# Delta rule with the keys convolved first, corner products and 32x32 transposes in its triangular inverse, and weight quarters set between the levels

## What is computed

```
proj = rms_norm(x) @ w_in                      # q, k, v, z, gates a and b, attention, index heads
qkv = silu(causal_short_conv(g_qkv, conv_w))   # 3072 channels, 4 taps
gq = l2_normalize(gq) * 128 ** -0.5 ; gk = l2_normalize(gk)
a_mat = where(strict, (k * beta) @ k.T * decay, 0)
sol = triangular_solve(a_mat + I, [v * beta, k * beta * exp(g_cum)])
qk = where(incl, q @ k.T * decay, 0)
v_new = u - w @ state ; o = q_dec @ state + qk @ v_new
state = state * exp(g_last) + k_dec.T @ v_new  # from chunk to chunk
o_gdn = rms_norm(o) * silu(z) ; merged = sigmoid(gate_a) * o_gdn + sigmoid(gate_b) * o_att
x = x + merged @ w_out
```

## Time and profile before

| | us |
|---|---|
| median of 3 runs (lowest to highest) | 950.84 (950.75 to 953.18) |
| the profiled execution | 952.35 |
| its span, first to last instruction | 950.5 |
| PE busy in it | 921.4 |
| DVE, ACT, POOL busy | 591.9, 451.3, 124.7 |

### The profile page before, as it was taken

The page is one execution under the profiler, slowest core; times in us unless marked ns, Lnnn a source line. Parts: engine busy times, 40 slices in busy tenths (PEclk is TensorE's granted clock), DMA queues, the critical chain, the costliest instruction groups (busy, mean ns, idle before and its releaser), DMA issues.

```text
span 950.5 us, 11857 instructions
## 1 busy us (share of the span) xinstructions
PE 921.4 (97%) x4691; PEld 771.8 (81%) x4691; DVE 591.9 (62%) x816; ACT 451.3 (47%) x654; POOL 124.7 (13%) x82
## 2 busy tenths in 40 slices
PE   8999999998998999999999999999998999999998
PEld 5887788876996888888887889888887888888886
DVE  4469978979456656654445745877774655555542
ACT  5265355963344544453335434753553455454531
POOL 0322112676601000000000002100000000000100
PEclk9999999999998999999999999999999999999999
DMA  7774542432312555555567645343541556554561
GB/s 268 191 247 137 177 133 89 143 124 70 95 45 85 164 193 178 177 177 177 179 192 276 208 143 174 138 133 120 181 144 44 165 164 196 183 177 133 200 221 67
DMA packets 83138, 149.87 MB, mean 158 GB/s; under 512 B 8320, under 2 KB 16048, under 8 KB 82960
## 3 DMA queue, kind: packets, MB, share of 16 engines
q1 hardware_dynamic: 79424, 144.52, 46.9%
q10 hardware_dynamic: 3040, 3.79, 1.1%
q0 software_dynamic: 624, 0.87, 0.8%
HBM read 147.72 MB, written 1.44 MB: 157 GB/s over the span
## 4 chain that ended last, share of the span: by engine, by line
PE 84%; DVE 7%; ACT 4%; DMA 3%; issue 1%; POOL 0%; SPq 0%; DVEq 0%; ACTq 0%
PE gemm L477 23%; PE gemm L479 23%; PE gemm L478 23%; PE mixbank L720 2%; DMA raw<-in_w_in_dram 2%; PE mixbank L612 2%; PE mixbank L587 2%; DVE w_lo L1482 1%; PE mixbank L493 1%; ACT w_hi L1019 1%; ACT junk L1175 1%; PE mixbank L825 1%; PE mixbank L598 1%; DVE mix L1599 1%; ACT mix L1187 1%
## 5 line engine op out<-in xcount | busy, mean ns | idle before, releaser
L1482 DVE TENSOR_TENSOR w_lo<-raw,w_hi 128x2048 fp32r<-128x2048 f32 (+3 forms) x131 | 287.6, 2209 | 177.5 <-ACT w_hi L1019 177.4
L477 PE MATMUL gemm<-w_hi,s_hi 128*128 128x512 f32 (+3 forms) x912 | 354.6, 389 | 11.8 <-DVE w_lo L1482 7.6
L479 PE MATMUL gemm<-w_hi,s_lo 128*128 128x512 f32 (+3 forms) x912 | 347.3, 381 | 0.0
L478 PE MATMUL gemm<-w_lo,s_hi 128*128 128x512 f32 (+3 forms) x912 | 347.1, 381 | 0.0
L1019 ACT ACTIVATE w_hi<-raw 128x2048 fp32r<-128x2048 f32 (+3 forms) x140 | 255.4, 1836 | 167.7 <-DMA raw<-in_w_in_dram 47.6
L477 PEld LDWEIGHTS gemm<-w_hi,s_hi 128*128 128x128 f32 x912 | 172.4, 189 | 46.5 <-issue 10.6
L479 PEld LDWEIGHTS gemm<-w_hi,s_lo 128*128 128x128 f32 x912 | 172.3, 189 | 32.9
L478 PEld LDWEIGHTS gemm<-w_lo,s_hi 128*128 128x128 f32 x912 | 172.6, 189 | 31.0 <-issue 0.5
L2165 POOL TENSOR_TENSOR sm<-sm 128x2 f32<-128x2 f32 (+4 forms) x14 | 29.1, 2077 | 514.4 <-DVE sm L1526 318.8
L2159 POOL TENSOR_TENSOR w_lo<-raw,w_hi 128x2048 fp32r<-128x2048 f32 x9 | 41.4, 4616 | 202.4 <-ACT w_hi L1019 202.4
L477 PE MATMUL gemm<-w_hi,hT_hi 128*128 128x512 f32 x128 | 50.6, 396 | 0.0
(11 more groups left out here) (300 smaller groups left out, 950.8 us busy)
## 6 DMA issues: line engine op xcount, KB each, us to landing
raw<-in_w_in_dram SPq DMA_DIRECT2D x40, 1024.0 KB, 5.1
raw<-in_w_mlp_up_dram SPq DMA_DIRECT2D x16, 1024.0 KB, 5.6
raw<-in_w_mlp_down_dram SPq DMA_DIRECT2D x16, 1024.0 KB, 5.1
raw<-in_w_gate_dram SPq DMA_DIRECT2D x10, 1024.0 KB, 5.1
raw<-in_w_up_dram SPq DMA_DIRECT2D x10, 1024.0 KB, 5.2
raw<-in_w_down_dram SPq DMA_DIRECT2D x10, 1024.0 KB, 5.2
raw<-in_w_out_dram SPq DMA_DIRECT2D x8, 1024.0 KB, 5.1
raw<-in_w_xkv_dram SPq DMA_DIRECT2D x8, 1024.0 KB, 5.2
```

The costliest lines, as they stand in the source:

```text
L477: nc.tensor.matmul(o, hi, wh, start=kt == 0, stop=False)
L478: nc.tensor.matmul(o, hi, wl, start=False, stop=False)
L479: last = nc.tensor.matmul(o, lo, wh, start=False, stop=kt == blk["kt"] - 1)
L1482: V.tensor_tensor(w_lo[:, s, 0:kn, 0:width], raw[:, s, 0:kn, 0:width], w_hi[:, s, 0:kn, 0:width].bitcast(F32), ALU.subtract)\
```

## The change

**Convolution.** `CONV_ORDER` puts the keys first, with a table of banks. The loop is written out. Decay rows are made early by PE (with a constant that gives the differences at once), the exponential is taken by ACT from PSUM, and POOL applies the mask. The turned keys are copied by DVE (`keys`), and ACT squares the copies. Queries aren't turned back: ACT squares them as they are, and 16 products with one column each sum them (`query_sums`). DVE makes `AT` (`inverse_rows`) amid the taps of v. The norm factors of the queries are a power of their own (`gdnq`).

```
+        CONV_ORDER = (4, 5, 6, 7, 0, 1, 2, 3, 8, 9, 10, 11)
+        CONV_BANK, DEC_BANK = (0, 1, 2, 0, 2, 1, 0, 2, 0, 2, 1, 2), (1, 0, 2, 1)
+        KK_BANK, KQ_BANK = (1, 3, 0, 3), (0, 1, 2, 0)
+        BACK_ORDER = (0, 1, 2, 3, 8, 9, 10, 11)
...
+            def turned_back(i):
+
+                s = BACK_ORDER[i]
+                e = CONV_ORDER[s]
+                pe.wait_ge(sem("gdn_y"), s + 1)
...
+            def query_sums():
+
+                pe.wait_ge(sem("gdn_q2"), 4)
+                pe.wait_ge(sem("gdn_at"), 4)
+                for p in range(4):
+                    for j in range(2):
+                        for t in range(NT):
+                            c = 8 * t + 2 * p + j
+                            last = nc.tensor.matmul(M[3][:, c:c + 1], Y2[:, p, j, P * t:P * t + P], cst[:, C_ONES:C_ONES + 1], start=True, stop=True)
+                last.then_inc(sem("gdn_qs"), 1)
...
+            pe.wait_ge(sem("gdn_kn"), 1)
+            turned_back(1)
+
+            pe.wait_ge(sem("gdn_y"), 4)
+            decay_rows(1)
+            pe.wait_ge(sem("gdn_dme"), 1)
+            turned_in(5)
+            fill(5)
+            pe.wait_ge(sem("gdn_kn"), 2)
...
+            taps(4)
+            silu(3)
+            keys(0)
+            taps(5)
+            silu(4)
+            keys(1)
+            taps(6)
+            silu(5)
```

```
+                        if (b, c) == (B_GA, 0):
+                            base_first()
+                        if (b, c) == (B_GA, 1):
+                            base_second()
+                        if (b, c) == (B_GA + 1, 0):
+                            base_return()
                         load(b, c)
-                    if b == B_GA + 1:
-                        base_blocks()
...
+            def corner(u, q, m, lv, step):
+
+                h = 1 << lv
+                even, odd = slice(2 * h * m, 2 * h * m + h), slice(2 * h * m + h, 2 * h * m + 2 * h)
+                cols, n = slice(64 * q + h * m, 64 * q + h * m + h), 4 * u + q
+                if step == 0:
+                    return nc.tensor.matmul(M[u][odd, cols], AT[even, n, odd], XI[even, n, even], start=True, stop=True)
+                return nc.tensor.matmul(M[u][even, cols], PS[odd, n, even], XT[odd, n, odd], start=True, stop=True)
+
+            for step, needed, made in ((0, "inv_x", "inv_p"), (1, "inv_pc", "inv_tp")):
+                for u in (0, 2):
+
+                    for v in (u, u + 1):
+                        pe.wait_ge(sem(needed), 4 * step + v + 1)
+                    for q in range(4):
+                        corner(u, q, 0, 5, step)
+                        corner(u + 1, q, 1, 5, step)
+                    for q in range(4):
+                        first = corner(u, q, 1, 5, step)
+                        second = corner(u + 1, q, 0, 5, step)
+                    first.then_inc(sem(made), 1)
+                    second.then_inc(sem(made), 1)
+            mm(B_GA, quarters=[2])
...
+                        for m in range(64 // h):
+                            even, cols = slice(2 * h * m, 2 * h * m + h), slice(2 * h * m + h, 2 * h * m + 2 * h)
+                            ins = V.tensor_scalar(XT[even, n, cols], half_bank(M[u], lv)[even, :, m, :], -1.0, None, ALU.mult)
+                    sig(ins, "inv_xt")
+                    if k < 2:
+
+                        dve.wait_ge(sem("inv_xt"), 4 * k + u + 1)
+                        if k == 0:
+                            ins = V.transpose(XI[:, n, :], XT[:, n, :])
+                        else:
+                            ins = V.transpose(XI[32:64, n, 0:32], XT[0:32, n, 32:64])
+                        ins.then_inc(sem("inv_x"), 1)
```

The high parts of both chunks of B_GA+1 now stand ahead of the four copies, the gate's tanh and two value copies too. On POOL the power of the queries and KBG, KD move behind the masks; on DVE the low parts of B_O come at other places of the tail:

```
             output_factors(0)
             times_z(0)
             output_norm(1)
+            split(B_O, 0)
             times_z(1)
             output_factors(1)
...
             sig(ins, "o_done")
             turn_lo(banks=range(2, 4))
+            split(B_O, 1)
             begin(B_O)
             residual(B_O, 0)
```

```
+            def index_scores(t, queries, banks):
+
+
+                ns = P * (t + 1)
+                for n, q in enumerate(queries):
+                    for par in range(2):
+                        last = nc.tensor.matmul(M[banks[par]][:, ns * n:ns * n + ns], iqT[64 * par:64 * par + 64, q, P * t:P * t + P],
                                                 ikT[64 * par:64 * par + 64, 0:ns], start=True, stop=True)
-                        if q == 3 or (t == 1 and q == 1):
+                        if q == queries[-1]:
                             last.then_inc(sem("scores"), 1)
+
+            index_scores(0, range(4), (0, 1))
+            index_scores(1, range(0, 2), (2, 3))
+            pe.wait_ge(sem("relu"), 2)
+            index_scores(1, range(2, 4), (0, 1))
...
-            mm(B_GA + 1, quarters=[2, 3])
+            mm(B_GA + 1)
...
-            for par in range(2):
-                for half in range(2):
-                    e = 2 * par + half
-                    for j in range(2):
+            for half in range(2):
+
+                for j in range(2):
+                    for par in range(2):
                         q = 2 * half + j
-                        last = nc.tensor.matmul(M[e][:, 256 * j:256 * j + 256], rkT[64 * par:64 * par + 64, q, 0:P],
+                        last = nc.tensor.matmul(M[2 * par + half][:, 256 * j:256 * j + 256], rkT[64 * par:64 * par + 64, q, 0:P],
                                                 rqT[64 * par:64 * par + 64, q, :], start=True, stop=True)
-                    last.then_inc(sem("ret_s"), 1)
-
-            for par in range(2):
-                pe.wait_ge(sem("ret_w"), par + 1)
-                for q in range(4):
-                    last = nc.tensor.matmul(M[par][:, P * q:P * q + P], rkT[64 * par:64 * par + 64, q, P:2 * P],
+                        if j == 1:
+                            last.then_inc(sem("ret_s"), 1)
+            mm(B_2 + 6)
+
+            pe.wait_ge(sem("ret_w"), 2)
+            for q in range(4):
+                for par in range(2):
+                    last = nc.tensor.matmul(M[2 * par][:, P * q:P * q + P], rkT[64 * par:64 * par + 64, q, P:2 * P],
                                             rqT[64 * par:64 * par + 64, q, P:2 * P], start=True, stop=True)
-                last.then_inc(sem("ret_s"), 1)
-            mm(B_2 + 6)
+                    if q == 3:
+                        last.then_inc(sem("ret_s"), 1)
             mm(B_2 + 7)
```

646 lines of the change are left out of this document (368 added, 278 removed).

## The result

| | before | after |
|---|---|---|
| median us | 951.14 (4 runs, 950.75 to 953.18) | 971.24 (4 runs, 970.54 to 972.49) |
| ratio to before, 95% interval | | 1.0205 (1.0191 to 1.0219) |
| profiled execution, span | 952.35, 950.5 | 971.86, 970.2 |
| PE busy | 921.4 | 919.8 |

The change makes the kernel 2.05% slower, about 20 us, where 4 were forecast. The page of the changed kernel: the chain of waits has 5 points less of PE and 4 more of DVE than in the earlier trace rows.

What follows compares the result with a forecast made beforehand. The prediction took PE, 84% of the chain of waits, as the bound. PE's work -12.5, waits +16.0, clock +2.7 and score products -2.1 gave +4.1 us: 954.9 us against the 950.84 median, range 945.5 to 962.

Steps and rivals of the forecast that it cites:

- DVE's list from 187 to 214: Convolution stage: DVE's taps, silus, copy, gate, inverse rows and small ones fill some 20.5 of 27 us.
- one fall of the clock, +2.7: Level 4's second step and the quarter behind it run at 1.2 GHz after a 3.7 us wait: +2.7 us.
- Rival (2): The clock falls in the convolution stage too, some 3 us for each of two falls: 960.9 us; chance 0.11.
- The ring: Convolution stage: round trip from key copy to next copy takes 6.9 us; PE waits 2.4, 2.4, 3.3, plus 0.4 ahead: 8.4.
- Later waits in the stage: Convolution stage, 187 to 214: PE waits in four places, together 9.8 us.
- The solve at 226.4: DVE comes to the solve at 226.4, against 226.09 before, so putting keys first gains it nothing.
- Corner products: Levels 5 and 6: 128 records of 32x32 and 64 of 64x64 cost +9.4 us, bounds 5.7 to 21.5.
- Query sums: PE's 16 one-column products, 32 records at 0.093 us each: +3.0 us.
- the work sum: PE's instructions without the clock: -1.8 - 3.5 - 14.3 + 9.4 + 3.0, in all -7.2 us.
- Rival (3): Levels 5, 6 and query sums: small products priced by weight columns; 949.2 us, 946.5 with the clock held; chance 0.25.
- The waits behind the solve: PE waits 2.0 (value rows), 3.7 (level 4), 2.3 (merge, B_O) and 1.3 (B_O's second chunk): 9.3 us.
- Scores: Index and retention score products on alternating row groups overlap: -1.0 and -1.1 us, together -2.1.

Runs made afterwards that it cites:

- e1_port: Changed kernel with one added wait: POOL's three low parts begin only after DVE has made its five small key factors; 959.99 us, ratio 1.0080.
- e3_both: Changed kernel with e1_port's wait and each of DVE's four key copies moved one step earlier; 955.86 us, ratio 1.0036.
- i2_late: h2_masks with B_GA+1's high and low parts moved behind level 6 and the first state products; 942.66 us, ratio 0.9910.
- h1_masks: f4_best with POOL's masks of level 4 ahead of its third and fourth query products; 948.40 us, ratio 0.9957.
- i1_late: h1_masks with B_GA+1's high and low parts moved behind level 6 and the first state products; 943.51 us, ratio 0.9907.
- g2_both: g1_early with ACT's third copy of value rows ahead of its part of the placement; 952.77 us, ratio 0.9999.
- f1_wide: e3_both with each of the 16 query sums 32 columns wide instead of one; 954.46 us, ratio 1.0010.
- g1_early: f4_best with the eleventh pair's channels turned in ahead of key products 2 and 3, and its taps earlier on DVE; 951.62 us, ratio 0.9977.
- h2_masks: g2_both with POOL's masks of level 4 ahead of its third and fourth query products; 948.55 us, ratio 0.9964.
- f2_order: e3_both with the query sums behind the eleventh quarter instead of ahead of it; 950.47 us, ratio 0.9979.
- f3_hi: e3_both with B_GA+1's high and low parts (ACT, DVE) behind level 4 instead of ahead of its copies; 953.12 us, ratio 1.0003.
- f4_best: e3_both with the edits of both f2_order and f3_hi; 945.48 us, ratio 0.9937.

## Why the prediction was wrong

The direction was right, the size not: +4.1 forecast, +20.1 measured, outside the range of 945.5 to 962.

**The step that failed: DVE's list from 187 to 214.** It has "and small ones, some 20.5 of 27". The small ones were the five factors, a copy and a scaling, put in at about their own durations, 1.3 in all (20.5 less 13.0, 0.7, 1.3 and 4.2). The five factors alone took 11.2 where they take 0.9 in e1_port, 10.3 more. What failed is that each instruction was priced alone and its neighbour on the other engine was not looked up. POOL's stretch there was in the plan: the change puts three low parts directly behind the power for which DVE's factors wait, so they meet by construction. And the trace of before has the case. These are DVE's and POOL's timelines of the kernel before, a place that the prediction didn't use:

```profile
239.01 1.25 DVE L1803 TENSOR_SCALAR sm<-sm 128x16 f32<-128x16 f32 x1
240.30 1.20 DVE L1804 SCALAR_TENSOR_TENSOR sm<-sm 128x16 f32<-128x16 f32 x1
241.42 0.16 DVE L1805 TENSOR_TENSOR sm<-sm 128x16 f32<-128x16 f32 x1
```

```profile
233.76 8.96 POOL L2249 TENSOR_TENSOR mix<-mix 128x512 f32<-128x512 f32 x4 [8.48 <-DVE mix L1801]
```

Two instructions of 16 columns last 1.2 us beside POOL's four and end with POOL's second and third (at 240.23 and 241.47); a third slips in between two of them and lasts 0.16. A row that is seven times as long as its twin is worth an explanation before its kind is used in a sum. The Trainium skill has the rule (SBUF — State Buffer, section on SBUF's two separate sides): VectorE and GpSimd share a pair of ports under an exclusive lock, held for the whole instruction, and a VectorE instruction with two SBUF inputs or in a fast two-port mode blocks against GpSimd. The trace agrees: the three waits end with POOL's instructions, and those that read PSUM are not held up. By the rule the price was to be had beforehand: up to one low part (4.6 us in the trace of before) for each factor that meets one.

**The second step that failed: one fall of the clock, +2.7.** The trace has six falls: behind the waits of 2.89 and 2.56, within the one of 11.56, in the query sums behind a wait of 1.51, and behind 2.83 and 2.79. Two slices of the changed kernel at the last one:

```profile
262.00:264.00 2.00, 0.00 (x0) 0.00 (x0) 2.00 (x1) 1.53 (x1) 2.00 (x2) 1.00 0.00 0
264.00:275.00 11.00, 10.30 (x42) 9.59 (x43) 9.16 (x10) 1.47 (x5) 9.44 (x3) 0.53 0.00 0
```

The granted clock was 0.50 for 37.5 us of this stage, and PE was busy in 30.5 of them, so half of that, 15.2 us, is what the clock cost; before it was 11.2 of 13.7 us, 5.6. The forecast had 5.3 less and 2.7 more; the trace has 9.6 more. (Work after, 146.7, less 15.2 is 131.5; work before, 145.7, less 5.6 is 140.1. So the instructions gave 8.6, where their prices below add up to 9.9; the 1.3 between is not accounted for.) Rival (2) named such falls for the convolution stage, where three of the six came behind its waits and one in the query sums; it had a chance of 0.11 and a price of 6 us. What failed is "in none of the shorter ones": the sum took from two long waits with a fall, and short ones without, that a wait of 3.7 was the border, though the stage had no wait between 0.75 and 3.76 us before and so no row on the lengths that came.

**Point by point.**
- The ring: forecast 6.9 a turn and 2.4, 2.4, 3.3 of waiting; measured 6.86 for the first (170.13 to 176.99), and waits of 2.08, 2.15 and 2.89. Right.
- Later waits in the stage: 9.8 in four places forecast; 0.66, 2.56, 11.56 and 1.51 measured, 16.3. Without the exclusion (e1_port) 0.43, 2.53, 1.18 and 2.00, so 6.1: without the exclusion these were forecast too long by 3.7.
- The solve at 226.4: it began at 239.6, behind the exclusion and the half clock. That keys first gain nothing there was right for the change as it stands (230.5 without the exclusion), but not for the idea: in e3_both, with the ring gone too, the solve began at 222.8, and in i2_late at 220.3, 5.8 earlier than before, of which about 1.1 comes from the index scores. DVE's first product of the solve in the changed kernel and in e3_both:

```profile
239.62 0.17 DVE L1975 TENSOR_TENSOR mix<-mix 128x15 f32<-128x15 f32 x1
```

```profile
222.84 0.17 DVE L1975 TENSOR_TENSOR mix<-mix 128x15 f32<-128x15 f32 x1
```

- Corner products, forecast 9.4 with a lower bound of 5.7: 6.1.

```profile
275.78 1.20 PE L830 MATMUL mixbank<-mix 32*32 32x32 f32 x64
277.32 1.25 PE L831 MATMUL mixbank<-mix 32*32 32x32 f32 x64 [0.33 <-ACT mix L1410]
281.43 1.90 PE L830 MATMUL mixbank<-mix 64*64 64x64 f32 x29
```

  32x32 products cost 0.019 a record, under my lower bound of 0.03; 64x64 cost 0.057, against 0.056 taken. The bound was for one at a time, and the edit writes the 32x32 ones in alternation between two corners. In the trace the two records of such a pair start 6 to 7 ns apart, and the next pair 32 ns after the first, so a pair runs side by side. No run has them one after the other on the same corner.
- Query sums, forecast 3.0: 3.7 for 32 records with the last drain, nearly all at full clock (h1_masks), so 3.6, and 5.3 in the changed kernel, most of it at half clock. By these prices the work sum is -1.8 - 3.5 - 14.3 + 6.1 + 3.6 = -9.9 without the clock, where the forecast had -7.2. Rival (3), small products cheaper than taken, was right for the corners: all 224 records average 0.043, under its mark of 0.050, and the work is 2.7 us less than taken. It drowned in the rest.
- The waits behind the solve: forecast 2.0, 3.7, 2.3, 1.3; measured 2.83, 2.79, 2.01, 1.04, and 0.33 at level 5. Right in place and cause, the second 0.9 shorter.
- Scores: -2.1 forecast, -1.7 alone; of it 0.6 rather than 1.1 from the retention scores, which already ran partly in pairs.

In sum, by the account of the stage: of its 15.9 us above the forecast, 5.1 are waits, 12.2 the clock (9.6 more instead of 2.6 less), and the instructions gave 1.4 more than taken. The experiment cuts it another way: the exclusion is worth 11.9 us of the 20.1. In its profile e1_port has 10.2 us less waiting between 187 and 226, and still 34.1 us at half clock, with PE busy in 33.8 of them; so what the exclusion cost there is the wait, and the half clock only moved. Of its four runs two have a mean clock of 0.986 and 0.988 instead of 0.981, so how much of the 11.9 is clock can't be told exactly. The waits without the exclusion were forecast too long and the cost of the clock far too low, and these two errors partly hid each other.

## What to carry to other kernels

Before an instruction is moved, look at what the other engine of a shared path runs at its new place. A 0.2 us VectorE instruction with its inputs in SBUF cost 4.5 us beside a GpSimd subtraction of that length, and a wait that keeps the two apart gave back 1.25%. Where PE is the bound, a wait in a stretch of narrow products was worth several times itself: the 1.5 us of waits at level 6 that i1_late takes out of h1_masks gave 4.8 us. Such waits are best closed last to first: one closed ahead of an unclosed one only moved it to where it cost more (g2_both), and the gain showed when the last was gone (i1_late, i2_late).

## What the hardware showed that I had not expected

- VectorE and GpSimd exclude each other for whole instructions and in both directions: 16 columns 4.49 us beside a low part of 4.5 (0.17 alone); GpSimd's 128x1024 product 3.94 beside VectorE's low part (1.90 alone).
- 64 records of 32x32 products on alternating corners take 1.20 us, 0.019 each, a sixth of the 0.112 of a full one.
- The granted clock fell behind a wait of 2.0 us (e3_both, ahead of level 4) where narrow products followed, and stayed at 0.50 for 17.1 us although PE was idle for under 2 of them; in h1_masks it fell behind waits of 1.00, 0.27 and 0.27. But no length of a wait decides: the same wait of 2.0 us ahead of block B_O has half clock behind it in the profiles of e3_both, f1_wide, g1_early, h2_masks and i1_late, and none in those of the changed kernel, f2_order, f3_hi, f4_best, g2_both, h1_masks and i2_late. What decides stays open: f1_wide didn't tell wait from width.
- Nine runs of one kernel differ by up to 13 us (941 to 954, f4_best), in step with the mean granted clock. A difference of 0.5% between two such kernels needs as many runs as these had, and the clocks beside them.
